# One transformer layer on one core: linear attention placed between gate products and convolution taps, and its output products ahead of the convolution's

## The reference, cut to what matters

```python
# convolution branch
u = conv_a * sigmoid(conv_g)
u = depthwise_conv(u, conv_w) + conv_b               # 31 taps, causal
u = silu((u - mean(u)) * rsqrt(var(u) + 1e-5) * ln_g + ln_b)
y_conv = u @ w_conv_out + b_conv_out

# linear attention branch, 4 heads, chunks of 64 tokens
cum = cumsum(log_sigmoid(f_lr @ w_gate_up + b) / 16)  # within a chunk
k_dec = k * exp(cum_end - cum)
kv[n] = k_dec[n].T @ v[n];  state[n] = exp(cum_end[n]) * state[n-1] + kv[n]
o = (q / sqrt(128)) @ state
o = o * rsqrt(mean(o * o, per head) + 1e-6) * norm_g * silu(r)
y_gla = o @ w_gla_out

merged = sigmoid(gate_a) * y_conv + sigmoid(gate_b) * y_gla
x1 = layer_norm(ALPHA * x + merged @ w_out + b_out)
```

## Time and profile before

| | us |
|---|---|
| median of 3 runs (1871.27 to 1871.55) | 1871.41 |
| the profiled execution | 1866.17 |
| its span | 1864.4 |
| TensorE busy with matmuls | 1432.7 (77%) |
| VectorE busy | 560.3 (30%) |
| ScalarE busy | 451.2 (24%) |
| GpSimd busy | 566.4 (30%) |
| granted TensorE clock, mean | 0.915 |

### The profile page before, as it was taken

How to read it: one execution, slowest core, us unless ns; L and a number is a source line. 1 busy time by engine, 2 the same in 40 slices (tenths; PEclk the granted TensorE clock), 3 DMA queues, 4 the chain that set the end, 5 groups by cost and what they waited for, 6 DMA issues and landing times.

```text
span 1864.4 us, 21403 instructions
## 1 busy us (share of the span) xinstructions
PE 1432.7 (77%) x9194; PEld 986.5 (53%) x9194; DVE 560.3 (30%) x874; ACT 451.2 (24%) x554; POOL 566.4 (30%) x151
## 2 busy tenths in 40 slices
PE   6998887865766567656775667564999689899897
PEld 6898886521332133312331233121899678899785
DVE  1997366000000000000000000002658942257602
ACT  3354531100000000000000000002347353534433
POOL 6786363000000000000000000002384738687782
PEclk9999999988998898889988898888799899899998
DMA  8453338899999999999999999999155333445450
GB/s 325 153 182 136 124 136 315 324 409 410 410 410 410 410 410 410 409 410 410 410 410 410 410 410 410 410 409 393 52 181 204 136 113 136 141 183 185 169 180 23
DMA packets 116576, 539.42 MB, mean 289 GB/s; under 512 B 4440, under 2 KB 8544, under 8 KB 108832
## 3 DMA queue, kind: packets, MB, share of 16 engines
q1 hardware_dynamic: 113232, 532.44, 73.1%
q0 software_dynamic: 1184, 3.94, 0.6%
q10 hardware_dynamic: 2096, 2.11, 0.4%
HBM read 537.41 MB, written 1.06 MB: 289 GB/s over the span
## 4 chain that ended last, share of the span: by engine, by line
DMA 40%; PE 32%; DVE 11%; SPq 7%; ACT 5%; issue 3%; POOL 2%; DVEq 0%; ACTq 0%
DMA ring<-in_w 39%; PE bank L547 26%; SPq L381 7%; PE bank L766 4%; DVE slab L1423 2%; POOL ring_parts L485 2%; ACT ring_parts L1008 2%; DVE slab L1427 1%; DMA ring<-in_units 1%; DVE slab L1508 1%; DVE rows_parts L1755 1%; DVE slab L1849 0%; DVE slab L1486 0%; PE bank L752 0%; DVE slab L1517 0%
## 5 line engine op out<-in xcount | busy, mean ns | idle before, releaser
L485 POOL TENSOR_TENSOR ring_parts<-ring,ring_parts 128x2048 fp32r<-128x2048 f32 x114 | 547.6, 4829 | 259.3 <-ACT ring_parts L1008 259.3
L766 PE MATMUL bank<-ring,slab 128*32 128x512 f32 x2016 | 335.5, 801 | 304.6 <-DMA ring<-in_w 303.7
L547 PE MATMUL bank<-slab_parts,ring_parts 128*128 128x256 f32 x3328 | 506.1, 288 | 27.5 <-DVE slab_parts L1438 14.2
L547 PEld LDWEIGHTS bank<-slab_parts,ring_parts 128*128 128x128 f32 x3328 | 464.9, 196 | 33.6 <-DVE slab_parts L1438 14.8
L766 PEld LDWEIGHTS bank<-ring,slab 128*32 128x32 f32 x2016 | 65.7, 133 | 563.4 <-DMA ring<-in_w 389.9
L499 POOL TENSOR_TENSOR slab_parts<-slab,slab_parts 128x1088 fp32r<-128x1088 f32 x1 | 2.5, 2494 | 946.9 <-ACT slab_parts L1157 946.9
L1008 ACT ACTIVATE ring_parts<-ring 128x2048 fp32r<-128x2048 f32 x114 | 211.6, 1908 | 114.3 <-PE bank L547 114.3
L1689 DVE TENSOR_TENSOR slab<-slab,bank 128x512 f32<-128x512 f32 x16 | 11.0, 687 | 624.4 <-PE bank L766 624.4
L547 PE MATMUL bank<-rows_parts,ring_parts 128*128 128x256 f32 x752 | 188.1, 287 | 0.0
L547 PE MATMUL bank<-ring_parts,slab_parts 128*128 128x512 f32 (+1 forms) x672 | 166.2, 398 | 15.2 <-POOL ring_parts L485 6.5
L547 PEld LDWEIGHTS bank<-ring_parts,slab_parts 128*128 128x128 f32 x672 | 129.8, 196 | 44.4 <-POOL ring_parts L485 8.2
(11 more groups left out here) (290 smaller groups left out, 916.1 us busy)
## 6 DMA issues: line engine op xcount, KB each, us to landing
ring<-in_w SPq DMA_DIRECT2D x190, 2048.0 KB, 23.7
ring<-in_units SPq DMA_DIRECT2D x59, 2048.0 KB, 8.0
slab<-in_w SPq DMA_DIRECT2D x2, 2048.0 KB, 14.9
ring<-in_units SPq DMA_DIRECT2D x2, 1024.0 KB, 14.1
slab<-bias_scratch ACTq DMA_DIRECT2D x2, 1024.0 KB, 8.0
slab<-in_xT SPq DMA_DIRECT2D x1, 1024.0 KB, 5.2
rows<-in_ln_g POOLq DMA_DIRECT2D x2, 512.0 KB, 8.8
slab<-in_x SPq DMA_DIRECT2D x1, 1024.0 KB, 4.9
```

What stands on the lines that cost most here:

```text
L485: g.tensor_tensor(r32(w), w, r32(high), ALU.subtract).then_inc(S("low_ready"), 1)
L547: return mm(out_, l, r, start=start and first, stop=stop and last)
L766: last = mm(b[CAP * j:CAP * j + CAP, :], xg[:, c, CAP * j:CAP * j + CAP], wt[:, j, i, :], start=c == 0, stop=c == DC - 1, tile_position=(0 ...
```

## The change

TensorE's products keep their number and shape; their order changes. `kdt` goes directly behind `r3`, then `ga0`, `ga1`, then `kv0` to `kv7`, then `ga2`, `ga3`, then `o0` to `o3`, then `gb0`, `gb1`, then `osum0`, `osum1` and `csum`, then `gb2`, `gb3`, then `csq`. `yg0` to `yg3` come ahead of `yc0` to `yc3`. The stored weights keep their order in DRAM (`STORED1`); the ring takes them in the new order.

```diff
-V_LAGS = (4, 12)
-GLU_LAG, GATE_LAG = 18, 29
+V_LAGS = (2, 4)
+KEY_LAGS = (6, 11, 16)
+GLU_LAG, GATE_LAG = 13, 26
...
-                if name == "yg1":
+                if name == "yc3":
...
-            wait_used(sp, "yg1")
+            wait_used(sp, "yg3")
+            early(2)
+            wait_used(sp, "yc1")
             early(0)
-            wait_used(sp, "yg3")
+            wait_used(sp, "yc3")
             early(1)
-            early(2)
-            sp.wait_ge(S("merged_ready"), 4)
+            wait_read(sp, "yc0", "yc1", "yc2", "yc3")
             early(3)
```

GpSimd now does its constants first, waits for the first half unit, and then issues the seven small loads:

```diff
+            pool.wait_ge(S("first_half_landed"), 16)
             pool.dma_start(w_flr[:], a["w_flr"]).then_inc(S("small_landed"), 16)
```

VectorE does the keys and states within the second half of the convolution, and takes the mean, the convolution's root and the attention's roots from PSUM, where ScalarE writes its square roots in place:

```diff
+            long_conv(1, n, {V_LAGS[0]: lambda: take_v(0), V_LAGS[1]: lambda: take_v(1), KEY_LAGS[0]: decay_keys,
+                             KEY_LAGS[1]: turned_keys, KEY_LAGS[2]: sum_states})
+            root = []
+            for j in range(2):
+                o = bank(f"osum{j}")
+                dve.wait_ge(S("osum_root"), j + 1)
+                v.reciprocal(o[:, 0:512], o[:, 0:512]).then_inc(S("o_step"), 1)
+                root.append(o)
             o = wait_full(dve, "csum")
-            read(ts(mean, o[:, 0:T], -1.0 / D, None, ALU.mult), "csum")
...
             for c in range(DC):
-                tt(chan(3)[:, c, :], chan(3)[:, c, :], mean, ALU.add).then_inc(S("centered"), 1)
...
+                ins = stt(chan(3)[:, c, :], o[:, 0:T], -1.0 / D, chan(3)[:, c, :], ALU.mult, ALU.add)
+            read(ins, "csum")
+            dve.wait_ge(S("o_step"), 2)
             for c in range(DC):
...
+                ins = stt(chan(10)[:, c, :], chan(10)[:, c, :], col("gla_g", c),
+                          root[c // 4][:, T * (c // 2 % 2):T * (c // 2 % 2) + T], ALU.mult, ALU.mult)
...
             tt(slab[:, 10, :], slab[:, 10, :], slab[:, 0, :], ALU.mult).then_inc(S("gla_ready"), 1)
             dve.wait_ge(S("gla_high"), 1)
             low_part(slab[:, 10, :], slab[:, 5, :], slab[:, 10, :]).then_inc(S("gla_low"), 1)

+            o = bank("csq")
+            wait_read(dve, "csum")
+            dve.wait_ge(S("csq_root"), 1)
+            v.reciprocal(o[:, 0:T], o[:, 0:T]).then_inc(S("conv_rstd"), 1)
+            dve.wait_ge(S("conv_rstd"), 1)
+            for c in range(DC):
+                ins = tt(chan(3)[:, c, :], chan(3)[:, c, :], o[:, 0:T], ALU.mult)
```

The step that scales `x` (two instructions of 128x1024) moves from behind the merging to between the `yg` and the `yc` outputs, and the merging is done in the bank of `yc`:

```diff
+                for m in range(2):
+                    c = 2 * j + m
+                    stt(o[:, T * m:T * m + T], o[:, T * m:T * m + T], col("b_co", c), chan(1)[:, c, :],
+                        ALU.add, ALU.mult).then_inc(S("yc_gated"), 1)
+                wait_read(dve, f"yg{j}")
+                dve.wait_ge(S("yc_gated"), 2 * j + 2)
+                read(tt(slab[:, 1, 512 * j:512 * j + 512], o[:], slab[:, 6, 512 * j:512 * j + 512], ALU.add), f"yc{j}")
```

More of the change, by code:

```diff
@@ L76, in _tasks @@
     names += [f"v{u}_{t}" for u in range(2) for t in range(2)] + ["q0", "q1"]
[L77 to L80, removed]
+    names += [f"r{j}" for j in range(4)] + ["kdt0", "kdt1", "ga0", "ga1"] + [f"kv{i}" for i in range(8)]
+    names += ["ga2", "ga3"] + [f"o{h}" for h in range(4)] + ["gb0", "gb1", "osum0", "osum1", "csum"]
+    names += ["gb2", "gb3", "csq"]
+    names += [f"yg{j}" for j in range(4)] + [f"yc{j}" for j in range(4)]
     names += [f"mix{u}_{t}" for t in range(2) for u in range(2)]
@@ L125 @@
 BANK = _bank_table()
-UNITS1 = ["g1", "a1", "g3", "a3", "k1", "v0_1", "v1_1", "q1", "r1", "r3", "ga1", "ga3", "gb1", "gb3",
-          "yc1", "yc3", "yg1", "yg3", "mix0_1", "mix1_1"]
+STORED1 = ["g1", "a1", "g3", "a3", "k1", "v0_1", "v1_1", "q1", "r1", "r3", "ga1", "ga3", "gb1", "gb3",
+           "yc1", "yc3", "yg1", "yg3", "mix0_1", "mix1_1"]
+UNITS1 = STORED1[:14] + ["yg1", "yg3", "yc1", "yc3"] + STORED1[18:]
 UNITS2 = (["lx1", "lx3", "lg_1", "lg_3", "vv", "qi1", "li3", "qq1", "qq3", "gc1", "gc3", "ya1", "ya3",
@@ L245, in states @@
             return slab[:, s, at + HV * h:at + HV * h + HV]
-        mean = slab[:, 10, 768:1024]
-        conv_root = slab[:, 10, 0:T]
         kiwi_high = slab[:, 4, 512:512 + DC * 136]
@@ L649, in _ @@
             chan_major(unit(), xTs, ["r2", "r3"])
-            chan_major(unit(), xTs, ["ga0", "ga1"])
-            chan_major(unit(), xTs, ["ga2", "ga3"])
-            pe.wait_ge(S("consts_ready"), CONSTS)
-            o = take_bank("csum")
-            for c in range(DC):
-                if c % 4 == 0:
-                    pe.wait_ge(S("conv_tap"), (4 * CONV_W + 2) * (c // 4 + 1))
-                last = mm(o[:, 0:T], ones[:], chan(3)[:, c, :], start=c == 0, stop=c == DC - 1)
-            full(last, "csum")
             pe.wait_ge(S("consts_ready"), CONSTS)
@@ L667, in _ @@
                 full(last, f"kdt{t}")
+            chan_major(unit(), xTs, ["ga0", "ga1"])
             wait_read(pe, "kdt0", "kdt1", "v0_0", "v0_1", "v1_0", "v1_1")
@@ L680, in _ @@
                     full(last, task)
-            chan_major(unit(), xTs, ["gb0", "gb1"])
-            o = take_bank("csq")
-            pe.wait_ge(S("csq_ready"), 1)
-            for c in range(DC):
-                last = mm(o[:, 0:T], ones[:], chan(2)[:, c, :], start=c == 0, stop=c == DC - 1)
-            full(last, "csq")
+            chan_major(unit(), xTs, ["ga2", "ga3"])
             wait_read(pe, "q0", "q1")
@@ L698, in _ @@
                 full(last, f"o{h}")
-            chan_major(unit(), xTs, ["gb2", "gb3"])
+            chan_major(unit(), xTs, ["gb0", "gb1"])
             for j in range(2):
@@ L708, in _ @@
                 full(last, f"osum{j}")
+            pe.wait_ge(S("consts_ready"), CONSTS)
+            o = take_bank("csum")
+            for c in range(DC):
+                if c % 4 == 0:
+                    pe.wait_ge(S("conv_tap"), (4 * CONV_W + 2) * (c // 4 + 1))
+                last = mm(o[:, 0:T], ones[:], chan(3)[:, c, :], start=c == 0, stop=c == DC - 1)
+            full(last, "csum")
+            chan_major(unit(), xTs, ["gb2", "gb3"])
+            o = take_bank("csq")
+            pe.wait_ge(S("csq_ready"), 1)
+            for c in range(DC):
+                last = mm(o[:, 0:T], ones[:], chan(2)[:, c, :], start=c == 0, stop=c == DC - 1)
+            full(last, "csq")
+            pe.wait_ge(S("gla_low"), 1)
+            chan_major(unit(), gla_parts, ["yg0", "yg1"])
+            chan_major(unit(), gla_parts, ["yg2", "yg3"])
             pe.wait_ge(S("conv_low"), 1)
```

150 lines of the change are left out of this document (67 added, 83 removed).

## The result

| | before | changed |
|---|---|---|
| median of the runs, us | 1871.48 (1871.27 to 1873.95, 4 runs) | 1849.61 (1846.5 to 1852.62, 4 runs) |
| profiled execution, us | 1866.17 | 1852.62 |
| its span, us | 1864.4 | 1850.9 |
| TensorE's first matmul, us | 14.20 | 9.02 |
| `a0`'s first matmul | 29.59 | 25.32 |

The ratio is 0.988, with a 95% interval of 0.9862 to 0.9898: 21.9 us faster, where 18.8 us were forecast (1852.6 us), inside the range of 1846 to 1862 us.

The account below looks back on a forecast made before the run. DMA's expert stream, begun by TensorE's first use, was taken as the bound, with TensorE bounding the mixer before it. 15.3 us (parts 1 to 5) + 3.5 us (start) = 18.8 us, giving 1852.6 us, range 1846 to 1862 us.

Parts of the forecast that it names:

- What bounds the kernel: DMA streaming expert weights, starting with TensorE's first use; TensorE bounds the mixer, whose savings reach the end one for one.
- Hidden anyway: Rival, chance 0.05: the expert stream is bound by when its early loads were issued; gain 0 to 3 us, 1870.
- Slower: Rival, chance 0.04: TensorE without gaps is granted less clock; at a mean of 0.88, 24 us longer, 1876 us.
- Part 1: TensorE's order: the 4.73 us gap before `gb0` goes; VectorE's waits in the taps cost nothing, on 11 us of cover.
- Part 2: Before `yg0`: a new 7.7 us gap replaces gaps of 7.52 and 6.64 us, with one slow restart instead of two.
- the rival in which it loses the turn: Chance 0.10: the attention's low part waits while GpSimd runs both halves of `yg3`; price 4.6 us, 1857.2.
- Restarts: TensorE's slow units behind gaps: 1.5 + 2.2 + 1.7 us go, one of 2.2 us comes; 3.2 us saved.
- Part 3: VectorE instructions with both inputs in SBUF wait for a whole GpSimd instruction; those reading a PSUM bank are not held up.
- Part 4: The convolution's second part runs under `yg`, `conv_low` ready with 15 us to spare; it and scaling `x` cost nothing.
- Part 5: End of the mixer: a gap of 2.3 us after `yc3` against 2.16 us, and the 1.03 us gap goes.
- Part 6: Small loads sent behind the first half unit: the start shifts about 3.5 us earlier, bounds 0 and 5.4.
- Sum: Gaps 12.1 us and restarts 3.2 us make 15.3 us; with 3.5 us from the start, 18.8 us.

Follow-up runs that it names:

- keys_behind_taps: The changed kernel with VectorE's keys and states moved from inside the convolution's taps to behind them; 1863.36 us, ratio 0.9956.
- small_first: The changed kernel with the seven small loads back at the head of GpSimd's queue; 1851.45 us, ratio 0.9914.
- act_order: The changed kernel with ScalarE's attention roots and high part moved ahead of its splits of yg1's and yg3's weights; 1839.72 us, ratio 0.9841.
- filled_gap: The changed kernel with 48 extra matmuls, result overwritten, in TensorE's gap before yg0; 1848.77 us, ratio 0.9875.
- act_warm: act_order with 15 extra matmuls on constants in TensorE's two router waits; 1835.27 us, ratio 0.9822.
- before_again: The kernel before, unchanged, run once more for a second profile; 1872.48 us (one run).

## Why the prediction was right, and where it was not

- **What bounds the kernel:** right. The first expert matmul came 16.8 us earlier and the chain's first long DMA wait 15.1 us earlier (348.66 to 333.57 us), with DMA idle before it. "Hidden anyway" is out, and the saving does reach the end one for one: from the first expert matmul to the first transpose behind the experts it was 970.7 us in both profiles of before and 970.7 to 971.0 us in eight of the other eleven (the exceptions are in the last section). "Slower" is out too: the granted clock was 1.00 from 140 to 190 us, where TensorE never stopped.
- **Part 1, TensorE's order and VectorE in the taps:** right. VectorE waited 14.99 us for the turned keys and ended its taps at 176.9 us, 3.6 us ahead of the 180.5 of the sum, about the earlier start; `csum` began at 187.1 us, so the cover was 10 us. `keys_behind_taps` shows what it costs without. One gap is missing from the list: the kernel before also waited 0.99 us in front of `kv0`, for VectorE's copy of the turned keys, and the changed kernel does not.
- **Part 2, the new gap:** 7.31 us against 7.7. Inversions 6.58 us (6.7 taken), centring 2.72 (3.3), scaling 3.22 (3.3), low part 3.12 with its wait for GpSimd (3.1). The rival in which it loses the turn did not happen: the low part took 3.11 to 3.15 us in all seven profiles with this order of ScalarE and VectorE.
- **Restarts:** 2.0 to 2.7 us for one behind a gap of 7.3 us in the two profiles of the changed kernel; taken 2.2.
- **Part 3, the PSUM operands:** the step that failed, though no term of the sum hung on it. The mechanism is as told, but I gave these operands a role in the new order that they do not have: GpSimd is idle from 195.7 to 206.3 us there, and taking them away costs 0.3 us of gap. The rows to see it were at hand. By the times of part 2, counted from `gb1` full, ScalarE has the first half of `yg1`'s split done at about 2.7 us and GpSimd's two instructions on it (9.6 us) end at about 12.3 us; the centring begins at 13.2 us, and GpSimd has nothing more until behind the scaling. The trace has 195.7 us for the one and 196.88 us for the other. And I did not price them alone in the old order, where they are worth 16 us, as much as the reordering.
- **Part 4:** right. The convolution's low part was ready at 223.4 us, TensorE was inside the 384 matmuls without a gap.
- **Part 5:** half right. The gap before `mix` is 2.42 us (2.3 taken). That of 1.03 us did not go: GpSimd's two instructions for `mix1_1` fell from 10.99 to 9.16 us, but TensorE's first 44 matmuls from 11.86 to 10.22 us as well, and 0.85 us of waiting is left. From the first `mix` matmul to the first transpose it is 1.8 us less (24.81 to 23.00 us), where the sum had 1.0.
- **Part 6, the start:** size off, 4.3 us instead of 3.5, within its bounds. ScalarE's split of `a1` began at 20.87 us, right behind the gates of `g0`; it did not wait for the landing, which I had put at 21.9 us at the latest. In time the gain is not settled (1.8 us by the medians of `small_first` and the changed kernel, 4.2 us in each of the two other pairs, 3.2 to 5.2 us at the mixer's end).
- **Sum:** 15.3 us for parts 1 to 5; measured 16.6 us in the first pair of profiles, and between 16.6 and 21.3 us over the two profiles of each. The first pair adds up: 15.3, and 1.0 for the gap left out, 0.8 for part 5, 0.4 for the smaller gap before `yg0`, less 0.6 for its dearer restart and 0.1 for the gap before `mix`, make 16.8. The 3.1 us by which the result beat the forecast are no more than the two profiles of one kernel differ by, and no row assigns them to a step.
- **Not in the forecast:** the router's 26.3 to 30.7 us. I used the profile of before as if its stretches without a change were fixed; they vary by as much as a part of the change.

## What to carry to other kernels

Before crediting a reordering and a change of operands separately, price each alone: two cures for one stall do not add up, and here a change to where three small tensors live gave, as far as these runs can tell, all that a rewritten schedule on four engines gave. A cure that is idle in one order can still be needed for the next step, as the operands seem to be in `act_order`, where GpSimd works while VectorE centres. When a chain of small steps ends at TensorE, look first at what stands between the steps on the engines that serve them (ScalarE's weight splits here, 6.5 us); moving them was worth some 8 us, while the PSUM operands, which shorten the steps, were worth 0.3 us of gap in the same order. Compare stretches that nothing has touched in two profiles of one kernel before reading a difference of 4 us into them.

## What the runs showed of the hardware that I had not expected

- The same 16 matmuls in the router took 1.98 us or 3.66 us in two profiles of one kernel, at a granted clock of 1.00 or 0.51, each time behind waits of 2.88 and 0.8 us; with the waits filled by matmuls whose result nobody uses they took 1.98 us (one profile).
- In three profiles (`keys_behind_taps`, `filled_gap`, `act_warm`) the granted clock from 600 to 900 us was 0.80, 0.78 and 0.78, against 0.86 in `before_again` and 0.89 in the others. Within these 300 us that cost nothing: DMA moved 410 GB/s in every profile. Over the whole of the experts, from their first matmul to the first transpose behind them, it was 974.3, 974.9 and 971.0 us, against 970.7 to 971.0 us in nine others and 972.6 us in the changed kernel's first profile. So two of the three were some 4 us longer; what tells them from the third is not shown.
- ScalarE and VectorE working in place in PSUM cost nothing extra: two roots 1.24 us (1.26 into SBUF), two inversions 6.58 us (6.55 for the same width in SBUF).
